# The last MLP of a three-layer kernel multiplies unnormed operand tiles, and the norm's factor is applied to the product

## The reference

```
h = rmsnorm(x, norm_mlp_w) * (1.0 + scale_f) + shift_f
x = x + gate_f * (jnp.square(jax.nn.relu(h @ w_up)) @ w_down)      # 1024 -> 4096 -> 1024
return rmsnorm(x, norm_final_w)
```

## Time and profile before

| | |
|---|---|
| runs | 1355.06, 1347.4, 1355.24 us; median 1355.06 |
| profiled execution | 1352.02 us, span 1350.1 us, mean granted clock 0.966 |
| TensorE, VectorE, ScalarE busy | 94%, 71%, 52% of the span |
| the last MLP, up tile 0 to the last down slab | 1144.16 to 1334.4 us |

### The profile page before, as it was taken

The page is one execution under the profiler, slowest core; times in us unless marked ns, Lnnn a source line. Parts: engine busy times, 40 slices in busy tenths (PEclk is TensorE's granted clock), DMA queues, the critical chain, the costliest instruction groups (busy, mean ns, idle before and its releaser), DMA issues.

```text
span 1350.1 us, 27191 instructions
## 1 busy us (share of the span) xinstructions
PE 1271.1 (94%) x9944; PEld 1235.0 (91%) x9944; DVE 957.2 (71%) x1728; ACT 698.0 (52%) x1077; POOL 28.8 (2%) x58
## 2 busy tenths in 40 slices
PE   6878899999999999999999989999999998999997
PEld 6867899999999999999999879899899997999997
DVE  4574578888788886778888888787876555555554
ACT  4325465555545445455555566666665334544442
POOL 0000000000000000000000000000000000000000
PEclk9889899999999999999999979999999998899998
DMA  6421356666467555856665525445336453455540
GB/s 262 125 63 63 134 179 205 207 210 222 168 234 261 194 208 223 266 169 208 217 215 179 182 91 192 141 155 171 124 126 199 159 187 125 142 186 186 182 160 31
DMA packets 71007, 234.66 MB, mean 174 GB/s; under 512 B 7056, under 2 KB 15376, under 8 KB 70304
## 3 DMA queue, kind: packets, MB, share of 16 engines
q1 hardware_dynamic: 63280, 203.87, 45.2%
q0 software_dynamic: 7664, 29.92, 6.7%
HBM read 232.69 MB, written 1.08 MB: 173 GB/s over the span
## 4 chain that ended last, share of the span: by engine, by line
PE 48%; DVE 31%; issue 10%; ACT 9%; DVEq 1%; DMA 0%; ACTq 0%; SPq 0%; PEldq 0%
PE ps L182 14%; PE ps L184 13%; PE ps L183 13%; DVE w_lo L174 13%; DVE arena L827 3%; ACT w_hi L169 3%; DVE arena L821 2%; DVE arena L829 2%; ACT arena L771 2%; PE ps L213 2%; DVE arena L1527 1%; DVE b_lo L850 1%; DVE arena L357 1%; ACT arena L565 1%; PE ps L1267 1%
## 5 line engine op out<-in xcount | busy, mean ns | idle before, releaser
L182 PE MATMUL ps<-a_hi,w_hi 128*128 128x256 f32 x1912 | 561.3, 294 | 9.4 <-DVE a_lo L1136 5.3
L174 DVE TENSOR_TENSOR w_lo<-w_raw,w_hi 128x1024 fp32r<-128x1024 f32 x381 | 462.1, 1220 | 142.8 <-ACT w_hi L169 140.5
L183 PE MATMUL ps<-a_lo,w_hi 128*128 128x256 f32 x1912 | 549.3, 287 | 0.0
L184 PE MATMUL ps<-a_hi,w_lo 128*128 128x256 f32 x1912 | 548.8, 287 | 0.0
L182 PEld LDWEIGHTS ps<-a_hi,w_hi 128*128 128x128 f32 x1912 | 375.1, 196 | 21.8 <-issue 14.8
L169 ACT ACTIVATE w_hi<-w_raw 128x1024 fp32r<-128x1024 f32 x381 | 386.7, 1046 | 13.9 <-DMA w_raw<-stream 7.2
L183 PEld LDWEIGHTS ps<-a_lo,w_hi 128*128 128x128 f32 x1912 | 375.8, 197 | 0.6 <-issue 0.2
L184 PEld LDWEIGHTS ps<-a_hi,w_lo 128*128 128x128 f32 x1912 | 375.4, 196 | 0.0
L182 PE MATMUL ps<-b_hi,w_hi 128*128 128x256 f32 x928 | 265.4, 286 | 8.0 <-DVE b_lo L850 4.1
L183 PE MATMUL ps<-b_lo,w_hi 128*128 128x256 f32 x928 | 262.5, 283 | 0.0
L184 PE MATMUL ps<-b_hi,w_lo 128*128 128x256 f32 x928 | 262.5, 283 | 0.0
(11 more groups left out here) (248 smaller groups left out, 1190.1 us busy)
## 6 DMA issues: line engine op xcount, KB each, us to landing
w_raw<-stream SPq DMA_DIRECT2D x381, 512.0 KB, 4.1
arena<-ada POOLq DMA_DIRECT2D x48, 512.0 KB, 5.5
c_hi<-cum_rows POOLq DMA_DIRECT2D x4, 1024.0 KB, 5.7
con<-consts SPq DMA_DIRECT2D x1, 1440.0 KB, 13.0
arena<-x SPq DMA_DIRECT2D x1, 1024.0 KB, 5.1
out<-arena SPq DMA_DIRECT2D x2, 512.0 KB, 3.0
arena<-c_rows POOLq DMA_DIRECT2D x1, 512.0 KB, 7.0
par<-params SPq DMA_DIRECT2D x1, 319.0 KB, 5.5
```

The costliest lines, as they stand in the source:

```text
L174: dve.tensor_tensor(w_lo[:, s % RING], w_raw[:, s % RING], w_hi[:, s % RING].bitcast(F32), ALU.subtract).then_inc(w_lo_ready, 1)
L182: pe.matmul(o, wh, xh, start=start, stop=False, skip_group_check=shared)
L183: pe.matmul(o, wh, xl, start=False, stop=False, skip_group_check=shared)
L184: return pe.matmul(o, wl, xh, start=False, stop=stop, skip_group_check=shared)
```

## The change

The operand of the last MLP becomes `c_hi`, `c_lo`, of `res` times g without the norm's factor, and 258 columns wide: columns 256 and 257 both hold `shift_f`. They are made during the output projection. The sums of squares stand between the matmuls of up tile 0. Each up product is evicted by VectorE, which multiplies it by `inv`, and copies column 256, the shift's product, to `up_shift`; ScalarE's relu reads that result from SBUF with `up_shift` as its bias. `high` and `hidden_of` now stand behind the second weight slab of a tile, not ahead of it. The sums of the MLP's norm go to PSUM bank 7.

```diff
-        c_hi, c_lo = sb("c_hi", [P, NT, SEQ], F32R), sb("c_lo", [P, NT, SEQ], F32R)
+        c_hi_wide, c_lo_wide = sb("c_hi", [P, NT, SEQ + 2], F32R), sb("c_lo", [P, NT, SEQ + 2], F32R)
+        c_hi, c_lo = c_hi_wide[:, :, 0:SEQ], c_lo_wide[:, :, 0:SEQ]
...
+        mlp_shift = mod[:, MOD[5][1]:MOD[5][1] + NT].unsqueeze(2).broadcast_to((P, NT, 2))
...
         def ssd_act(act):
             act_inv(act, 4)
             mod_act(act, 4)
+            act.activation(c_hi_wide[:, :, SEQ:SEQ + 2], mlp_shift, ACT.Copy).then_inc(shift_hi, 1)
             hi_ahead(act, S_DT + 3)
...
             for m in range(NT):
                 hi_ahead(act, S_WOUT + m + 3)
+                act.wait_ge(res_ready, NT * 5 + m + 1)
+                act.activation(c_hi[:, m], res[:, m], ACT.Copy, scale=eff_scale[:, 1, m:m + 1]).then_inc(a_hi_ready, 1)
                 square(act, 5, m)
...
         def ssd_vec(dve, step):
             mod_vec(dve, step, 4)
+            dve.wait_ge(shift_hi, 1)
+            dve.tensor_tensor(c_lo_wide[:, :, SEQ:SEQ + 2], mlp_shift, c_hi_wide[:, :, SEQ:SEQ + 2].bitcast(F32), ALU.subtract).then_inc(shift_ready, 1)
             lo_ahead(dve, S_DT + 3)
...
+            def lower(m):
+                dve.wait_ge(a_hi_ready, NT * 5 + m + 1)
+                dve.scalar_tensor_tensor(out=c_lo[:, m], in0=res[:, m], scalar=eff_scale[:, 1, m:m + 1], in1=c_hi[:, m].bitcast(F32),
+                                         op0=ALU.mult, op1=ALU.subtract).then_inc(a_ready, 1)
+
             for m in range(NT):
-                lo_ahead(dve, S_WOUT + m + 3)
                 dve.wait_ge(w_used, S_WOUT + m + 1)
                 dve.scalar_tensor_tensor(out=res[:, m], in0=ps[:, 4 + (m + 2) % 4, 0:SEQ], scalar=mod[:, 2 * NT + m:2 * NT + m + 1], in1=res[:, m],
                                          op0=ALU.mult, op1=ALU.add).then_inc(res_ready, 1)
+                if m < NT - 1:
+                    lo_ahead(dve, S_WOUT + m + 3)
+                lower(m)
+            lo_ahead(dve, S_WOUT + NT + 2)
...
         def mlp_pe(pe):
             def up_tile(n, it=None, each=None):
-                slab_gemm(pe, up_at(n), ps[:, 4 + n % 3, 0:SEQ], a_hi, a_lo, it, 6, each=each)
+                slab_gemm(pe, up_at(n), ps[:, 4 + n % 3, 0:SEQ + 2], c_hi_wide, c_lo_wide, it, 6, each=each)
...
-            for k in range(NT):
-                sum_squares(pe, 5, k)
+            pe.wait_ge(shift_ready, 1)
+            pe.wait_ge(res_ready, 6 * NT - 1)
+            up_tile(0, each=operand_and_sums(pe, 5))
+            up_tile(1)
             spread_inv(pe, 5)
-            up_tile(0, each=ready(a_ready, 5 * NT)(pe))
-            up_tile(1)
...
         def mlp_act(act):
-            act_inv(act, 5)
-            mod_act(act, 5)
             def relu_of(n, it=None):
-                act.wait_ge(w_used, val(up_at(n) + 1, it, 6))
+                act.wait_ge(up_out, val(n + 1, it, 3))
...
-                act.activation(relu[:, n % 3], ps[:, 4 + n % 3, 0:SEQ], ACT.Relu).then_inc(relu_ready, 1)
+                act.activation(relu[:, n % 3], up_m[:, n % 3], ACT.Relu, bias=up_shift[:, n % 3:n % 3 + 1]).then_inc(relu_ready, 1)
...
                 hi_ahead(act, up_at(n) + 3, it, 6)
+                if n == 0:
+                    act_inv(act, 5)
                 relu_of(n, it)
-                high(n, it)
                 if n >= 2:
                     hi_ahead(act, down_at(n - 2) + 3, it, 6)
+                high(n, it)
...
         def mlp_vec(dve, step):
-            mod_vec(dve, step, 5)
+            def evict(n, it=None):
+                dve.wait_ge(w_used, val(up_at(n) + 1, it, 6))
+                if n >= 3:
+                    dve.wait_ge(relu_ready, val(n - 2, it, 3))
+                dve.tensor_tensor(up_m[:, n % 3], ps[:, 4 + n % 3, 0:SEQ], inv[:, :], ALU.mult)
+                dve.tensor_copy(up_shift[:, n % 3:n % 3 + 1], ps[:, 4 + n % 3, SEQ:SEQ + 1]).then_inc(up_out, 1)
...
                 lo_ahead(dve, up_at(n) + 3, it, 6)
-                hidden_of(n, it)
+                if n == 0:
+                    vec_inv(dve, step, 5, EPS_B)
+                    dve.wait_ge(inv_ready, 6)
+                evict(n, it)
                 if n >= 2:
                     lo_ahead(dve, down_at(n - 2) + 3, it, 6)
+                hidden_of(n, it)
                 low(n, it)
```

## The result

The changed kernel takes 1356.95 us (median of 20 runs, 1353.24 to 1359.75). The kernel before, run on the same chip, takes 1351.97 us (20 runs, 1347.4 to 1355.33). The ratio is 1.0042, 95% interval 1.003 to 1.0055: slower by 0.42%, some 5.7 us by the ratio and 5.0 between the medians. The time lies within the range, but the difference is clear of the noise, and the forecast of 1355 beside a shown 1355.06 had none.

A forecast was written before the change was run, and what follows sets the result against it. TensorE bounds the MLP's loop before; after the change a VectorE-ScalarE ring would. The start's 13.0 us gain is given back, 2.2 us later, plus 0.2 for copies: +2.4 us, median put at 1355 us, range 1343 to 1365.

The forecast's parts named there:

- sum of +2.4 us: Whole kernel: 2.2 us later at the last MLP's end plus 0.2 for the shift's copies, on the profiled 1352.0 us.
- the ring: Last MLP's loop: eight steps of VectorE and ScalarE waiting on each other, 6.20 us a tile against TensorE's 5.76.
- The start: Last MLP's start: TensorE no longer waits for the norm, so up tile 2 ends 13.0 us earlier.
- rival 3: Last MLP's start does not gain, through a falling clock or late c_lo: about 1365 us, chance 0.04.
- two turns in three: Last MLP's loop: share of turns with the long hand-over from hidden to its high part, giving a leg of 0.51 us.
- Rival 2: Handoffs in the loop dearer than in straight code, 0.18 us more at three places: ring 6.74, 1371 us, chance 0.09.
- The rest: Outside the last MLP: the shift's two copies cost 0.2 us in the state-space part; broadcasts and second scale vector nothing.
- The place of the median: Whole kernel: run median 3.0 us above the profiled execution, so the forecast median was put at 1355 us.
- Rival 1: Last MLP's loop: the ring does not close, TensorE stays the bound; 12.2 us earlier, 1340 us, chance 0.10.
- Rival 4: VectorE starts an instruction only behind the full end of the one before: 6.47 us a tile, 1363 us, chance 0.05.

The follow-up runs named there:

- e1: The changed kernel with VectorE's eviction moved ahead of the remainder of the tile's first weight slab (tiles 1 to 31): 1339.83 us, ratio 0.9907 to the kernel before.
- e6: The kernel before with only the wide operand buffers, the cum_rows broadcasts in 1 KB pieces and the shift's two copies: 1350.51 us, ratio 1.0001.
- e4: The changed kernel with two more one-column copies in each eviction, ahead of the one that releases relu: 1359.48 us, ratio 1.0063 to the kernel before.

## Why the prediction was right or wrong

The forecast said no change, and the kernel is slower, clear of noise. Two steps of the prediction failed. The last one turned a sum of +2.4 us into a median equal to that of before. The other is a term of the sum, the ring's 6.20 us a tile, where 6.33 were measured, above all by the copy's hand-over to relu, put at 0.19 us where the loop takes 0.26; it makes some 3 us. Each is about half of the error. The mechanism itself, the closed ring, is what the runs show.

**The start: right.** From the projection's end to eviction 0 it forecast 1143.4 - 1132.75 = 10.7 us; it took 1145.12 - 1134.76 = 10.4. The clock stayed at 1.00, so rival 3 falls, and the 13.0 us of gain agree with what e1 keeps: 13.3 in the MLP. The missing 0.3 is up tile 0 with its sums, 1134.76 to 1141.19, 6.43 for the 6.76 read elsewhere.

**The ring: right in kind, 0.13 us a tile too short.** Its steps against the tile shown above, start to start:

| leg | forecast | measured |
|---|---|---|
| high of hidden to high A | 0.32 | 0.32, in the third tile of a turn 0.40 |
| high A to remainder A | 1.08 | 1.07 to 1.08 |
| remainder A to eviction | 1.14 | 1.15 |
| eviction to copy to relu | 0.33 + 0.19 | 0.33 + 0.26 |
| relu to high B | 0.40 to 0.41 | 0.42 |
| high B to remainder B | 1.08 | 1.07 |
| remainder B to square | 1.14 | 1.15 |
| square to high of hidden | 0.51 | 0.53 |
| sum | 6.20 | 6.30, 6.30, 6.40: mean 6.33 |

The mis-sized step is the one that took the copy's hand-over from the earlier trace rows, which stand in straight code, that is, outside the hardware loop. In straight code it is 0.18 here (1145.46 to 1145.64), as forecast, and in the loop 0.26 (1197.32 to 1197.58). The same instructions in the same order show it whole. These are two evictions of the change ahead of the hardware loop, tiles 2 and 3:

```profile
1153.25 0.42 DVE L1740 TENSOR_TENSOR arena<-ps,inv 128x256 f32<-128x256 f32 x1
...
1159.39 0.42 DVE L1740 TENSOR_TENSOR arena<-ps,inv 128x256 f32<-128x256 f32 x1
```

They are 6.14 apart, where those in the loop are 6.30. The two hand-overs from VectorE to ScalarE, copy to relu and square to high part, make the 0.16.

The dearer hand-over stood in the trace of before, and I misread it. Of the two tiles in the earlier trace rows the first, with a square's hand-over of 0.46, is tile 4, the last one ahead of the hardware loop, and the second, with 0.54, is the first inside it. In before all 24 tiles of the loop have 0.53 or 0.54 and the eight outside it 0.45 or 0.46, so "two turns in three" was wrong, and the surcharge belonged on the copy's leg too. Rival 2 was true of its kind (a hand-over is dearer in the loop), at 0.07 us and not 0.18. Not every hand-over pays: a weight slab's high part to its remainder is 1.07 to 1.08 in both places. The rest of the 0.13 is 0.03 from the turn's boundary and 0.03 net from the other legs. Eviction 0 to the end took 1341.29 - 1145.12 = 196.2 us where 193.2 was forecast, 3.0 more: 24 loop tiles at 0.13 make 3.1, and the five straight tiles at 6.14 take 0.3 back.

**The rest: 0.2 was put, none was seen** (e6, which can't resolve 0.2). With the start 0.3 shorter and the ring 3.0 longer, the MLP came out at +4.9 where the sum had +2.2.

**The place of the median: wrong.** My sum was above before's profiled execution. I set it at 1355, which was the shown median of three runs of before, 1355.06, and so forecast no difference at all. Added to either base, the profiled 1352.0 or the median 1355.06, the 2.4 gives 1354.4 or 1357.5; I took the difference from one and the comparison from the other. Twenty runs put before at 1351.97, beside its profiled 1352.0. The sum itself said slower by 2.4 us; the measured number is 5.7, interval 4.1 to 7.4. This error and the ring's point the same way. That 1355 still lies only 2.0 us from the measured 1356.95 is luck: the base was 3.1 too high and the difference 5.0 too small.

**The other rivals.** Rival 1 did not happen, but its arithmetic did: with the ring opened, 12.2 us were forecast and e1 gained 0.93%, 12.6 us. Its argument, engines only half busy, was no argument: from 1200 to 1318 us VectorE and ScalarE are busy for 57% and 45% in the change, and for 63% and 49% in e1, where nothing is lost. Rival 4, the next VectorE instruction only behind the full end of the one before, is refuted for these forms by the loop itself: 0.33 behind a pass of 0.42 and 1.15 behind one of 1.23, as in the earlier trace rows. The Trainium skill (VectorE: DVE Perf Modes, The DRAIN you can't avoid) says that the next operation does not start until the pipe is empty, and goes on that one that is not held starts earlier; rival 4 left the second half out. The first half alone, read as the end of the record, would make the three legs 0.09 longer each, and the measurement decides against that reading.

Open: why a hand-over costs 0.07 to 0.08 more in the loop. The waits there are against a register's value, outside against a constant; that this is the reason was not tried, and it would have to explain why the weight slabs' hand-over pays nothing.

## What to carry to other kernels

Where two in-order engines hand work to each other twice in a round, follow the circle of waits and add up its legs from start to start; with no step left waiting for the bottleneck, that sum is the pace, however idle the two engines look (here busy for 57% and 45%). Put the step that waits for the bottleneck ahead of prefetch work in its engine's list: here one moved call turned a loss of 0.4% into a gain of 0.9%. And take each leg's price from the same kind of place, loop from loop, and its length from the spacing of starts, not from the duration of one.

## What was not expected of the hardware

- One-column VectorE copies from the accumulators start 0.065 us apart, though the record of each is 0.15 (e4).
- A hand-over from VectorE to ScalarE is dearer inside the hardware loop than in straight code by 0.07 to 0.08 us: 0.26 for 0.18, and 0.53 for 0.45. In before so is the one back, relu to square: 0.50 for 0.42.
- Behind a pause of 0.3 us TensorE's first matmul has a record of 0.39 us instead of 0.28, and the second starts 0.23 behind it instead of 0.12. Waits of 8.6 us on its weight load stood for a loss of 24 x (6.33 - 5.76) = 13.7 us.
